# A two-block transformer step on one core: the Fourier group transform split into one cosine and one sine product, and two modulation slots loaded later

## The reference, cut to what matters

```python
def fourier_mix(u):
    b, s, _ = u.shape
    ug = u.reshape(b, s, FOURIER_GROUPS, FOURIER_GROUP_DIM).astype(jnp.float32)
    f = jnp.fft.fftn(ug, axes=(1, 3), norm="ortho")
    return jnp.real(f).reshape(b, s, D_FOURIER).astype(u.dtype)
...
mod = jnp.einsum('bd,dm->bm', c_act, w_ada[l]) + b_ada[l]
shift_m, scale_m, gate_m, shift_f, scale_f, gate_f = jnp.split(mod, N_MOD, axis=-1)
...
y_a = jnp.einsum('bsk,kd->bsd', fourier_mix(u_f), w_fourier[l])
```

## Time and profile before

| | |
|---|---|
| Median of three runs | 1303.47 us (1301.85 to 1303.57) |
| Profiled execution, its own time | 1301.74 us |
| Span of the profile | 1299.7 us (2.0 us of its time lie around it) |
| PE busy | 980.9 us, 75% |
| DVE busy | 386.9 us, 30% |
| ACT busy | 248.9 us, 19% |
| DMA | 496.43 MB, mean 382 GB/s |
| Chain that ended last | DMA 56%, PE 39% |
| Head, up to the first expert's first matmul | 234.4 us |

### The profile page before, as it was taken

How to read it: one execution, slowest core, us unless ns; L and a number is a source line. 1 busy time by engine, 2 the same in 40 slices (tenths; PEclk the granted TensorE clock), 3 DMA queues, 4 the chain that set the end, 5 groups by cost and what they waited for, 6 DMA issues and landing times.

```text
span 1299.7 us, 15644 instructions
## 1 busy us (share of the span) xinstructions
PE 980.9 (75%) x6764; PEld 558.1 (43%) x6764; DVE 386.9 (30%) x591; ACT 248.9 (19%) x387; POOL 21.3 (2%) x47
## 2 busy tenths in 40 slices
PE   9999999978465666666666656756565766899998
PEld 8899999323121221212121212212121222487988
DVE  5888866210000110000010101000000110388875
ACT  4444434001000000000000000000000000376764
POOL 2000200000000000000000000000000000000000
PEclk9999999988887787688797778787787888999999
DMA  9998999999999999999999999999999999994331
GB/s 336 389 389 310 320 381 417 396 421 433 428 433 429 436 431 425 429 438 426 433 435 427 428 437 433 425 434 433 426 433 435 433 423 425 387 342 139 126 130 33
DMA packets 73292, 496.43 MB, mean 382 GB/s; under 512 B 4858, under 2 KB 27018, under 8 KB 53792
## 3 DMA queue, kind: packets, MB, share of 16 engines
q1 hardware_dynamic: 70928, 489.11, 91.5%
q0 software_dynamic: 2080, 6.55, 1.6%
q10 hardware_dynamic: 240, 0.11, 0.0%
HBM read 494.71 MB, written 1.06 MB: 381 GB/s over the span
## 4 chain that ended last, share of the span: by engine, by line
DMA 56%; PE 39%; SPq 2%; DVE 1%; ACT 1%; issue 1%; DVEq 0%
DMA ring<-in_w_down_e 21%; DMA ring<-in_w_up_e 18%; DMA ring<-in_w_gate_e 16%; PE psum L769 7%; PE psum L770 7%; PE psum L771 7%; PE psum L1272 7%; PE psum L1304 5%; SPq L572 1%; PE psum L1237 1%; SPq L585 1%; DMA ring<-in_w_in 1%; PE psum L1362 1%; PE psum L1230 1%; PE psum L1248 0%
## 5 line engine op out<-in xcount | busy, mean ns | idle before, releaser
L1272 PE MATMUL psum<-ring,arena 128*32 128x512 f32 x2048 | 303.5, 741 | 182.3 <-DMA ring<-in_w_up_e 109.6
L1272 PEld LDWEIGHTS psum<-ring,arena 128*32 128x32 f32 x2048 | 70.6, 129 | 375.5 <-issue 175.2
L1304 PE MATMUL psum<-ring,arena 128*32 128x512 f32 x912 | 151.7, 820 | 97.4 <-DMA ring<-in_w_down_e 97.4
L1304 PEld LDWEIGHTS psum<-ring,arena 128*32 128x32 f32 x912 | 39.8, 140 | 194.9 <-issue 142.5
L1964 DVE TENSOR_TENSOR ring_r<-ring,ring_r 128x2048 fp32r<-128x2048 f32 x48 | 108.7, 2287 | 30.9 <-ACT ring_r L1552 30.8
L1723 ACT ACTIVATE arena<-psum 128x512 f32<-128x512 f32 x16 | 9.6, 598 | 533.2 <-PE psum L1272 533.2
L769 PE MATMUL psum<-ht_hi,ring_r 128*128 128x256 f32 x384 | 109.4, 285 | 0.0
L770 PE MATMUL psum<-ht_lo,ring_r 128*128 128x256 f32 x384 | 108.0, 281 | 0.0
L771 PE MATMUL psum<-ht_hi,ring_r 128*128 128x256 f32 x384 | 107.5, 280 | 0.0
L2330 DVE TENSOR_TENSOR arena<-psum,arena 128x512 f32<-128x512 f32 x30 | 19.3, 686 | 278.2 <-PE psum L1304 278.2
L1552 ACT ACTIVATE ring_r<-ring 128x2048 fp32r<-128x2048 f32 x48 | 90.5, 1911 | 21.9 <-PE psum L771 14.8
(11 more groups left out here) (313 smaller groups left out, 951.1 us busy)
## 6 DMA issues: line engine op xcount, KB each, us to landing
ring<-in_w_gate_e SPq DMA_DIRECT2D x23, 4096.0 KB, 33.3
ring<-in_w_up_e SPq DMA_DIRECT2D x22, 4096.0 KB, 32.8
ring<-in_w_down_e SPq DMA_DIRECT2D x21, 4096.0 KB, 33.7
ring<-in_w_up_e SPq DMA_DIRECT2D x16, 2048.0 KB, 36.4
ring<-in_w_in SPq DMA_DIRECT2D x30, 1024.0 KB, 10.3
ring<-in_w_gate_e SPq DMA_DIRECT2D x14, 2048.0 KB, 36.0
ring<-in_w_down_e SPq DMA_DIRECT2D x14, 2048.0 KB, 36.9
ring<-in_w_ada SPq DMA_DIRECT2D x16, 1024.0 KB, 9.8
```

The costliest lines, as they stand in the source:

```text
L1272: last = mm(psum[32 * g:32 * g + 32, b, :].rearrange("s (q c) -> s q c", c=4), cur[h][:, k, :], w[:, g // 2, :, g % 2 * 4:g % 2 * 4 + 4], ...
L1304: last = mm(psum[32 * q:32 * q + 32, 2 + n, :], act_t[:, f % 4, (f // 4) * CAP:(f // 4 + 1) * CAP], w[:, kk, n * BANK:(n + 1) * BANK], sta ...
```

## The change

1. The table `dftg` loses the minus-sine third; it holds cosine and sine.
2. The group unit on TensorE makes, for each group, the cosine sums into columns 0 to 128 of the bank and the sine sums into columns 129 to 255, one matmul each.
3. ScalarE copies the 2x127 sine sums of a bank into `sin_sum`, and frequencies 0 and 128 into a new whole-valued `fm`. VectorE subtracts and adds: frequencies 1 to 127 are cosine minus sine, and the mirrored ones, written backwards, cosine plus sine. The second of them frees the bank.
4. `fm_hi` and `fm_lo` are made from `fm` in unit b0, behind its splits and adds. ya0 waits for `fm_lo` by `st_ready`, whose counts rise by two.
5. `ADA_PER_UNIT` gives units 7 and 8 one modulation slot in place of two, and units 13 and 14 two in place of one. So slot (1,7), which was loaded ahead of ga0's weights, now is loaded ahead of ya0's.

```diff
-    dft_group = np.concatenate([np.cos(b), -np.sin(b), np.sin(b)], 1) / np.sqrt(P)
+    dft_group = np.concatenate([np.cos(b), np.sin(b)], 1) / np.sqrt(P)
...
-ADA_PER_UNIT = {6: 2, 7: 2, 8: 2, 9: 1, 10: 1, 11: 1, 12: 2, 13: 1, 14: 1, 15: 2, 16: 1}
+ADA_PER_UNIT = {6: 2, 7: 1, 8: 1, 9: 1, 10: 1, 11: 1, 12: 2, 13: 2, 14: 2, 15: 2, 16: 1}
...
+        fm = shaped(cat_flat[:, 0:D], k=FG, s=SEQ)
+        sin_sum = shaped(xr_flat[:, 0:FG * (FREQ - 2)], g=FG, s=FREQ - 2)
...
                             to, g = bank(2 * (u % 2) + j, c=2, s=SEQ)[:, c, :], 2 * j + c
-                            for mirrored, cols in ((False, slice(0, FREQ)), (True, slice(FREQ, SEQ))):
-                                for part in range(2):
-                                    half = ab[:, g, part * FREQ:(part + 1) * FREQ]
-                                    w = part * (2 if mirrored else 1)
-                                    last = mm(to[:, cols], dftg[:, w * P:(w + 1) * P], half[:, FREQ - 2:0:-1] if mirrored else half,
-                                              start=(part == 0), stop=(part == 1))
+                            mm(to[:, 0:FREQ], dftg[:, 0:P], ab[:, g, 0:FREQ], start=True, stop=True)
+                            last = mm(to[:, FREQ:SEQ], dftg[:, P:2 * P], ab[:, g, FREQ + 1:2 * FREQ - 1], start=True, stop=True)
...
                 elif name in ("ya0", "ya1"):
-                    await_read(pe, free, head_u["group"])
+                    pe.wait_ge(st_ready, 2)
...
                 elif name == "group":
                     for j in range(2):
+                        gs, both = slice(2 * j, 2 * j + 2), bank(b + j, c=2, s=SEQ)
                         await_bank(act, "head", u, j)
-                        f(fm_hi[:, 2 * j:2 * j + 2, :], bank(b + j, c=2, s=SEQ), ACT.Copy).then_inc(fm_hi_ready, 1)
+                        f(sin_sum[:, gs, :], both[:, :, FREQ:SEQ], ACT.Copy)
+                        f(fm[:, gs, 0:FREQ:FREQ - 1], both[:, :, 0:FREQ:FREQ - 1], ACT.Copy).then_inc(fm_kept, 1)
                 elif name in ("b0", "b1"):
+                    if name == "b0":
+                        for j in range(2):
+                            group = head_u["group"]
+                            act.wait_ge(free[head_pair(group) + j], reads_before(free, group) + 1)
+                            f(fm_hi[:, 2 * j:2 * j + 2, :], fm[:, 2 * j:2 * j + 2, :], ACT.Copy).then_inc(fm_kept, 1)
...
                 elif name == "group":
                     for j in range(2):
-                        dve.wait_ge(fm_hi_ready, j + 1)
-                        rest(fm_lo[:, 2 * j:2 * j + 2, :], bank(b + j, c=2, s=SEQ), fm_hi[:, 2 * j:2 * j + 2, :], free[b + j])
+                        gs, cos_sum = slice(2 * j, 2 * j + 2), bank(b + j, c=2, s=SEQ)[:, :, 1:FREQ - 1]
+                        dve.wait_ge(fm_kept, j + 1)
+                        V.tensor_tensor(fm[:, gs, 1:FREQ - 1], cos_sum, sin_sum[:, gs, :], ALU.subtract)
+                        V.tensor_tensor(fm[:, gs, SEQ - 1:FREQ - 1:-1], cos_sum, sin_sum[:, gs, :], ALU.add).then_inc(free[b + j], 1)
...
                 elif name in ("b0", "b1"):
+                    if name == "b0":
+                        for j in range(2):
+                            dve.wait_ge(fm_kept, 2 + j + 1)
+                            rest(fm_lo[:, 2 * j:2 * j + 2, :], fm[:, 2 * j:2 * j + 2, :], fm_hi[:, 2 * j:2 * j + 2, :], st_ready)
```

8 lines of the change are left out of this document (4 added, 4 removed).

## The result

| kernel | median | runs | profiled span |
|---|---|---|---|
| before | 1302.92 us | 6 (1300.96 to 1304.69) | 1299.7 us |
| after | 1312.33 us | 6 (1310.87 to 1313.16) | 1309.0 us |

The ratio is 1.0070, with a 95% interval from 1.0058 to 1.0083: the changed kernel is slower by 9.4 us, where 9.7 had been forecast (a median of 1313.2, measured 1312.33).

What follows compares the result with a forecast made beforehand. Experts bound by DMA, head by TensorE, whose delay reaches the end in full: -1.8 + 7.4 + 2.3 + 1.8 = +9.7 us on a median of 1303.5, forecast 1313.2 us, 0.7% slower; range 1308 to 1316.5.

Steps and rivals of the forecast that it cites:

- The group unit, -1.8: TensorE's group unit ahead of b0: eight matmuls fewer let b0 start 1.8 us earlier, bounds 0 and 1.8.
- VectorE's new work, at most 3.4: VectorE's four new instructions: at most 3.4 us if backwards writing costs double, offset by two adds given up, cost 0.
- Sum 1, +7.4: TensorE between ga0 and ga1: modulation sum 1 waits for slot (1,7)'s add, now behind ya0's split, 7.4 us.
- The clock, +2.3: TensorE after the wait at sum 1: half clock for a mean 4.6 us, half lost, 2.3 us; bounds 0 and 2.9.
- gb0, +1.8: TensorE at gb0's start: two adds for one between VectorE's splits make it wait 1.8 us, bounds 0 and 2.3.
- The sum: All terms at the issue of the experts' second pair of loads, at 235.56: -1.8 + 7.4 + 2.3 + 1.8 = +9.7 us.
- In full at the end: From the head through the experts: a delay reaches the end in full, a gain up to about 2.5 us.
- The range: Whole kernel: 1308 to 1316.5 us, said to take in the lower rival, the terms' bounds and about 1 us between runs.
- the clock stays up: Rival, TensorE in the head: the wait comes but the clock stays at 2.4 GHz; +7.4, 1310.9 us, chance 0.12.
- Absorbed: Rival, head: the delay is hidden behind DMA and the end does not move; 1303.5 us, chance 0.05.
- Add in time: Rival, sum 1: the seventh add is done before TensorE needs it, leaving only -1.8; 1301.7 us, chance 0.06.
- More waits: Rival, yb0 or `w_o`: a late slot holds TensorE another 4 us or so; 1317 us, chance 0.05.

Runs made afterwards that it cites:

- e1: The changed kernel with the slot table of the kernel before, so only the group transform is changed; median -0.4 us against before, ratio 0.9987 to 1.0007.
- e4: The changed kernel with another slot table: one slot each in units 7 and 8, two in b1 and ga0, one in units 13 and 14; 1298.66 us.
- e10: The kernel before, old group transform, with one slot each in units 7 and 8 and two each in b1 and ga0; 1301.23 us.
- e3: The changed kernel with modulation sum 1 moved one unit later on TensorE, ahead of ya0 instead of ga1; 1301.33 us.
- e7: The changed kernel with the add for slot (1,7) put ahead of ya0's split on VectorE, instead of behind it; 1306.94 us.
- e2: The kernel before with the changed kernel's slot table, so only the slots are moved; 1317.87 us.
- e9: The changed kernel with 30 additional unused 128x128 matmuls on TensorE ahead of the wait for modulation sum 1; 1310.74 us.
- e8: The changed kernel with one modulation slot fewer in ya1 and one more in yb0; 1310.8 us.
- e5: The changed kernel with 60 additional unused 128x128 matmuls on TensorE ahead of the wait for modulation sum 1; median +13.0 us against before.
- e6: The kernel before with 45 additional unused 128x128 matmuls on TensorE ahead of modulation sum 1; median +8.6 us against before.
- e11: The kernel before, unchanged, run once more for a second profile; hand-over +0.16 us, no median given (one run).
- e12: The changed kernel with the edits of e7 and e8 together; 1305.66 us.

## Why the prediction was right

The mechanism was right in each of its steps, one of its sizes (the clock's) was too large, and an effect that it did not have, the pitch, came on top. Point by point, the term, its forecast and what it measured:

- **The group unit, -1.8.** Measured -1.81 (75.35 against 77.16). Both conditions held: v1 was read out by 74.6 (73.95 + 0.68), earlier than the 75.0 I worked out, and b0 followed the last matmul at once. e1 shows the lower bound of 0, and e4 against e10 shows 1.7.
- **VectorE's new work, at most 3.4.** Four instructions of 0.41 us, whether written forwards or backwards; 1.6 in all, hidden as said.
- **Sum 1, +7.4.** Measured 7.36 of waiting; from ga0's last matmul to sum 1 it is 7.64 us against 0.21 before, so +7.43. e3 took the wait away and e7 most of it, by moving sum 1 on TensorE or one add on VectorE; e2 has it at the same length with the old group transform. Two details did not come as written: the page names "issue" and not the add of line 2048 as what ended the wait, and the slot was issued at 96.97, at the end of c1 and not by its middle. Neither bears on the wait.
- **The clock, +2.3.** Right that it falls, too large: 3.2 us of half clock past the restart, 1.4 us lost by e9. I had taken the mean of three stretches of the experts; this one was as short as the shortest of them. In e8, behind the same wait, it was 4.2 us or more and cost 0.4 us more.
- **gb0, +1.8.** The wait is 1.96 us, and in e8, with one add ahead of gb0's splits, it is gone. That such a wait is "short enough to leave the clock alone" held in the changed kernel's profile and in e9's, but not in those of e2, e5 and e7, where it cost about 1.5 us more. That it held in the changed kernel's profile is luck.
- **The sum.** -1.81 + 7.43 + 1.44 + 1.96 = +9.0 us. The pitch, which no term had, takes off 0.83 from b0 to ga0 and gives back 0.17 ahead of gb0 and 0.50 in the 288 matmuls from gb0 on. That is +8.9, and the hand-over measured +8.88. The forecast was 0.8 above that, nearly all of it the clock's term, and the median came out 0.5 above the hand-over; that 9.7 and 9.4 lie so close is in part luck.
- **In full at the end.** Span +9.3, median +9.4. e6 confirms it for a delay of another cause: 9.28 at the hand-over, 9.6 in the span, 8.6 in the median. Over all kernels the median's change lies between 1.6 below and 2.8 above that of the hand-over, so "in full" is shown for a delay of 9 us, not for each microsecond. For gains the prediction had a cap of about 2.5 us: e4's 2.77 at the hand-over went through whole, and no run gained more, so where the cap lies stays open.
- **The range.** The highest of all bounds, +13.8, makes 1317.3; the range stopped at 1316.5, without a reason given. It did not matter here.

The rivals: that the clock stays up (1310.9) is what e9 makes happen, at 1310.74. "Absorbed" falls with the result itself and with e6; what spoke for it was also read a little high, since the fourth slice of the head has DMA at 8 and not at nine tenths. "Add in time" describes e3 and e4, not the change. "More waits" did not come.

## What to carry to other kernels

Before an instruction is moved behind another in a queue, look up whether that other one waits for the very engine that will wait for the moved one: here an add of 2.35 us, moved behind a split that hangs on the waiting engine's last matmul, cost 7.4 us, and exchanging the two gave back 4.8. In this kernel the stage that feeds the DMA-bound one handed on its delay nearly in full, however busy DMA looked, and the issue where the second stage's first place comes free shows it in one row. When a change has one part that gains and one that only makes room for it, try other ways of making room: with three tables of slots the same group transform came out at +9.4, -0.4 and -4.1 us.

## What the runs showed of the hardware that I had not expected

- **The pitch of TensorE's 128x256 matmuls in products of three has several levels** at full clock: 0.1200 and 0.1178 us in most stretches, held for over 50 us (e4 from 122.1 to 178.4). It is 1.8%, 0.8 us over b0 to ga0, and small edits elsewhere switch it. From gb0 on it goes with the wait there: the next 288 matmuls take 33.88 or 33.89 us in the eight profiles in which TensorE did not wait at gb0, and 34.37 to 34.39 in the three in which it waited 0.9 to 2 us at full clock (after, e3, e9). Between b0 and ga0 it does not go with a wait: before and e11 have the long pitch there without one. What sets it stays open.
- **Half clock behind short waits.** Of seven waits of 1.96 to 2.60 us in dense work, three left the clock at 1.00 (gb0 in after and e9, sum 1 in e7) and four drew it to 0.50 for up to 3.6 us (gb0 in e2, e5, e7; sum 1 in e12). After, e5 and e9 have the same instructions around gb0 and differ only in idle matmuls that end 25 us or more before it; e7 and e12 have the same instructions of TensorE, VectorE and ScalarE up to sum 1. In both sets the clock went both ways, so a term for it is a chance, not a number.
- **A 128x254 VectorE subtraction or addition from PSUM takes 0.41 us** also where it writes with a step of -1 (line 2158 beside line 2157 above).
